# Stage norms of a six-stage fp32 model kernel: inverse deviation by Ln and Exp on ScalarE instead of Sqrt on ScalarE and reciprocal on VectorE

## The reference

```python
def rms_norm(x, g):
    y = xf * lax.rsqrt(jnp.mean(xf * xf, axis=-1, keepdims=True) + NORM_EPS)
    return (y * g)
...
    x = x + pool_mixer(rms_norm(x, pool_norm[j]), ...)          # conv_mixer, mla_mixer alike
    return rms_norm(x, final_norm)                              # end of the first block
...
    h = rms_norm_2(x, mix_pre_norm[l])
    x = x + rms_norm_2(hybrid_token_mixer(h, ...), mix_post_norm[l])
    h = rms_norm_2(x, ffn_pre_norm[l])
    x = x + rms_norm_2(conv_glu_ffn(h, ...), ffn_post_norm[l])
```

## Time and profile before

| | |
|---|---|
| median of 3 executions | 2356.09 us (2353.81 to 2356.2) |
| the profiled execution, its own time | 2356.29 us |
| its span, first to last instruction | 2354.5 us |
| mean granted TensorE clock | 0.981 |
| TensorE busy | 2269.4 us (96%) |
| VectorE busy | 1206.3 us (51%) |
| ScalarE busy | 886.3 us (38%) |
| GpSimd busy | 1031.4 us (44%) |
| instructions | 32284 |

### The profile page before, as it was taken

The page is one execution under the profiler, slowest core; times in us unless marked ns, Lnnn a source line. Parts: engine busy times, 40 slices in busy tenths (PEclk is TensorE's granted clock), DMA queues, the critical chain, the costliest instruction groups (busy, mean ns, idle before and its releaser), DMA issues.

```text
span 2354.5 us, 32284 instructions
## 1 busy us (share of the span) xinstructions
PE 2269.4 (96%) x10448; PEld 1816.3 (77%) x10448; DVE 1206.3 (51%) x1573; ACT 886.3 (38%) x1546; POOL 1031.4 (44%) x753
## 2 busy tenths in 40 slices
PE   8999999999999999999999999989999887999996
PEld 6788888888888887777887888776896565777785
DVE  7832234444432635555267223496754348888613
ACT  4343343344343434444333443334423323323322
POOL 5654444544544444443456544443200032555553
PEclk9999999999999999999999999999999889999998
DMA  3332323233222222111322322222100021222332
GB/s 133 98 99 98 98 91 99 96 98 98 98 96 96 95 93 72 54 63 36 99 90 89 107 98 93 101 89 72 55 1 1 1 72 45 90 97 89 102 104 98
DMA packets 53643, 194.46 MB, mean 83 GB/s; under 512 B 6080, under 2 KB 6336, under 8 KB 53568
## 3 DMA queue, kind: packets, MB, share of 16 engines
q1 hardware_dynamic: 52560, 191.13, 24.8%
q10 hardware_dynamic: 1008, 2.33, 0.3%
HBM read 191.34 MB, written 2.10 MB: 82 GB/s over the span
## 4 chain that ended last, share of the span: by engine, by line
PE 49%; issue 35%; POOL 15%; DVE 1%; POOLq 1%; ACT 0%; ACTq 0%; DVEq 0%
POOL w_lo L569 15%; PE proj L626 13%; PE proj L627 13%; PE proj L628 13%; PE aux L771 1%; PE proj L796 1%; PE proj L725 1%; PE proj L727 1%; PE proj L726 1%; PE aux L774 1%; PE aux L782 1%; PE proj L753 0%; PE proj L755 0%; PE proj L754 0%; PE proj L743 0%
## 5 line engine op out<-in xcount | busy, mean ns | idle before, releaser
L569 POOL TENSOR_TENSOR w_lo<-w_stage,w_hi 128x512 fp32r<-128x512 f32 x716 | 990.4, 1392 | 1226.1 <-ACT w_hi L1152 1225.5
L1152 ACT ACTIVATE w_hi<-w_stage 128x512 fp32r<-128x512 f32 x716 | 437.1, 627 | 761.9 <-PE proj L628 706.3
L626 PE MATMUL proj<-xh,w_hi 128*128 128x512 f32 x1696 | 672.6, 397 | 19.0 <-POOL w_lo L569 16.9
L627 PE MATMUL proj<-xl,w_hi 128*128 128x512 f32 x1696 | 662.0, 390 | 0.0
L628 PE MATMUL proj<-xh,w_lo 128*128 128x512 f32 x1696 | 661.8, 390 | 0.0
L626 PEld LDWEIGHTS proj<-xh,w_hi 128*128 128x128 f32 x1696 | 319.3, 188 | 106.0 <-POOL w_lo L569 34.1
L628 PEld LDWEIGHTS proj<-xh,w_lo 128*128 128x128 f32 x1696 | 319.1, 188 | 67.6
L627 PEld LDWEIGHTS proj<-xl,w_hi 128*128 128x128 f32 x1696 | 319.5, 188 | 66.8 <-issue 2.4
L626 PE MATMUL proj<-act_h,w_hi 128*128 128x512 f32 (+1 forms) x864 | 337.7, 391 | 0.6 <-POOL w_lo L569 0.6
L627 PE MATMUL proj<-act_l,w_hi 128*128 128x512 f32 (+1 forms) x864 | 336.9, 390 | 0.0
L628 PE MATMUL proj<-act_h,w_lo 128*128 128x512 f32 (+1 forms) x864 | 336.9, 390 | 0.0
(11 more groups left out here) (313 smaller groups left out, 2413.4 us busy)
## 6 DMA issues: line engine op xcount, KB each, us to landing
w_stage<-stream SPq DMA_DIRECT2D x358, 512.0 KB, 3.3
out<-x_res SPq DMA_DIRECT2D x4, 512.0 KB, 2.6
x_res<-x SPq DMA_DIRECT2D x2, 512.0 KB, 8.3
consts_sb<-consts ACTq DMA_DIRECT2D x1, 832.0 KB, 4.4
x_res<-x ACTq DMA_DIRECT2D x1, 512.0 KB, 7.4
x_res<-x SPq DMA_DIRECT2D x1, 256.0 KB, 3.3
x_res<-x ACTq DMA_DIRECT2D x1, 256.0 KB, 5.1
pos_i<-pos ACTq DMA_DIRECT2D x1, 256.0 KB, 2.7
```

Of the source, the lines that this page charges most:

```text
L569: pool.tensor_tensor(w_lo[:, at, :], w_stage[:, at, :], w_hi[:, at, :].bitcast(F32), ALU.subtract).then_inc(stage_free, 1)
L626: pe.matmul(o, w_hi[:, slot, cols], hi, start=(b == 0), stop=False)
L627: pe.matmul(o, w_hi[:, slot, cols], lo, start=False, stop=False)
L1152: act.activation(w_hi[:, u % RING, :], w_stage[:, u % RING, :], ACT.Copy).then_inc(hi_done, 1)
```

## The change

All nine places of `deviation` compute exp(-0.5 * ln(sum/D + eps)) on ScalarE. ScalarE's Ln writes std (or r_final), a new semaphore log_done orders the Exp behind it, the Exp writes rstd (or r_final in place) and raises std_done. VectorE's nine reciprocals are gone; its wait on std_done stays. Ahead of each wait for the sum ScalarE runs an Ln of one element per partition (warm).

```diff
                 if ahead:
                     his(4)
+                act.activation(warm[:, :], ones[:, 0:1], ACT.Ln)
                 if twice:
                     stds.up()
                     act.wait_ge(stat_done, stds.n)
-                    act.activation(std[:, :], aux[:, 1, :], ACT.Sqrt, bias=con("eps2"), scale=1.0 / D).then_inc(std_done, 1)
+                    act.activation(std[:, :], aux[:, 1, :], ACT.Ln, bias=con("eps2"), scale=1.0 / D).then_inc(log_done, 1)
+                    act.wait_ge(log_done, logs.up())
+                    act.activation(rstd[:, :], std[:, :], ACT.Exp, scale=-0.5).then_inc(std_done, 1)
                     stds.up()
                     act.wait_ge(stat_done, stds.n)
-                    act.activation(r_final[:, :], aux[:, 0, :], ACT.Sqrt, bias=con("eps"), scale=1.0 / D).then_inc(std_done, 1)
+                    act.activation(r_final[:, :], aux[:, 0, :], ACT.Ln, bias=con("eps"), scale=1.0 / D).then_inc(log_done, 1)
+                    act.wait_ge(log_done, logs.up())
+                    act.activation(r_final[:, :], r_final[:, :], ACT.Exp, scale=-0.5).then_inc(std_done, 1)
                     return
                 stds.up()
                 act.wait_ge(stat_done, stds.n)
-                act.activation(std[:, :], aux[:, 0, :], ACT.Sqrt, bias=con("eps"), scale=1.0 / D).then_inc(std_done, 1)
+                act.activation(std[:, :], aux[:, 0, :], ACT.Ln, bias=con("eps"), scale=1.0 / D).then_inc(log_done, 1)
+                act.wait_ge(log_done, logs.up())
+                act.activation(rstd[:, :], std[:, :], ACT.Exp, scale=-0.5).then_inc(std_done, 1)
...
                     stds.up()
                     dve.wait_ge(std_done, stds.n)
-                    link(dve.reciprocal(rstd[:, :], std[:, :]))
...
                 dve.wait_ge(std_done, stds.n)
-                link(dve.reciprocal(rstd[:, :], std[:, :]))
...
                     if c == 0:
                         dve.wait_ge(std_done, stds.n)
-                        link(dve.reciprocal(r_final[:, :], r_final[:, :]))
```

More of the change, by code:

```diff
@@ L411, in program @@
         std_done = sem("std_done")
+        log_done = sem("log_done")
         prod_done = sem("prod_done")
@@ L1139, in _ @@
             unit, tile = Count(), Count()
+            logs = Count()
             sqs, hs, stds, als, prods, silus, gates, xs = (Count() for _ in range(8))
```

## The result

The changed kernel was faster by more than forecast. In the first six executions of each kernel it took 2342.01 us (2341.6 to 2347.8) and the kernel before 2355.12 us: ratio 0.995, 95% interval 0.9937 to 0.9963, a gain of 13.1 us where 4.5 were forecast, and outside the range of 2347.0 to 2355.5. Over the whole study the changed kernel ran 20 times (median 2343.24) and the kernel before 90 times (median 2355.83): 12.6 us. The profiled execution took 2341.6 us, span 2339.4, granted clock 0.983.

A forecast was written before the change was run, and what follows sets the result against it. TensorE, busy 96% of the span, was taken as the bound. Gains of 1.45 + 1.45 + 1.8 + 1.0 less losses of 0.3, 0.7 and 0.2 gave 4.5 us: 2351.6 against 2356.09, range 2347 to 2355.5.

The forecast's parts named there:

- The price of a place: At each norm, from Ln's start to the first use of rstd: 2.72 us instead of 4.17, so rstd 1.45 earlier.
- at the end and behind the mixer: Norms at the kernel's end and behind the mixer: rstd comes earlier, a gain of 1.45 us at each.
- rival D: A switch of table sets costs another 1.28 us in whole-tile paths; slower, 2362.5 us; chance 0.05.
- rival E: The change doesn't do what it says, or one table load serves both functions; given no chance.
- pool0, pool1, conv, mla, mixer start: Norms of these stages: gain 1.0 us in pool0; losses 0.3 in pool1, 0.7 in conv, 0.2 in mixer; mla 0.
- Rival B: GpSimd's pairs do not give gains back: pool0 gives 2.7, pool1, mixer and ffn 1.4 each; 2345 us; chance 0.11.
- C: ScalarE's later weight units starve TensorE more: mixer 1.5, conv 1.2, pool1 and mla 0.5 each; 2354 us; chance 0.09.
- ffn: Norm of the ffn stage: earlier rstd offset by GpSimd's pair holding up VectorE; 0, bounds -0.3 and +1.4 us.
- r_final in chunk 0: First attention pair: TensorE's 1.83 us wait for softmax probabilities queued behind VectorE's reciprocal goes; gain 1.8 us.
- Rival A: In the chunks, TensorE's full clock returns sooner without the wait; worth 1 to 3.5, say 2.5 us: 2349.1; chance 0.20.
- P: Theory from the experiments: whether the clock falls at chunk 0 depends on when TensorE's short waits come, not on the reciprocal.

The follow-up runs named there:

- before_late: The kernel before plus extra matmuls filling TensorE's idle times at chunk 0 and in and behind the last chunk, no other change: 2347.23 us.
- after_late: The changed kernel plus extra matmuls filling TensorE's idle times at chunk 0 and in and behind the last chunk: 2335.68 us.
- all_but_r_final: The changed kernel with Sqrt and VectorE's reciprocal kept for r_final alone: 2351.62 us.
- after_again: The changed kernel as it is, run again for a second profile and more executions: 2345.66 us.
- before_again: The kernel before as it is, run again for a second profile: 2350.17 us in one execution.
- first_four: The kernel before with Ln and Exp at pool0, conv, mla and pool1 alone: 2355.18 us.
- before_pad1: The kernel before with the first head's products for wt made twice, 0.9 us more TensorE work just ahead of chunk 0: 2351.73 us.
- six_late: The changed kernel with Sqrt and reciprocal kept at conv, mla and pool1, and extra matmuls in TensorE's idle times at chunk 0 and the last chunk: 2334.05 us.

## Why the prediction was wrong

**The price of a place: right.** 2.73 measured for 2.72; 1.43 at the end and behind the mixer for 1.45; none of the new loads has a gap above 0.02 us. That settles rival D: the 1.38 us of drain in the Trainium skill, ScalarE: Activation LUTs, section What ACT_TABLE_LOAD costs, shows nowhere here, and the two loads of every place exclude rival E. The 13 more loads are there (72 against 59).

**pool0, pool1, conv, mla, mixer start: right in kind and nearly in size.** pool0 gave 1.3 by the load and 0.2 to 0.3 by the earlier first tile, 1.5 for my 1.0; the first mark itself scatters by 1 to 2 us between profiles of one form (28.4 to 29.6 with the reciprocal, 27.1 to 29.0 without), so the 1.98 of the two profiles is no better measure. pool1 lost 0.2 for 0.3. Conv lost 0.92 for 0.7, the same in every profile of either form. Rival B is refuted in pool0 by the 3.53 us behind the pair, and C came only at conv. The mixer's first tiles started 1.7 us later behind their mark, and by chunk 0 nothing of that was left.

**ffn: mis-sized.** From ffn's mark to the end's, eight profiles with the reciprocal take 362.94 on average, twelve without it 361.75: 1.2 us, where I took 0 with 1.4 as the bound. The traces show a third of it: GpSimd's pair does hold up VectorE's next steps, but by 1.05 of the 1.45 us (0.81 and 1.54 us where the kernel before has 0.55 and 0.75), so the first prod starts 10.68 us behind the mark, not 11.09, and TensorE's long wait ends 0.4 earlier. The rest comes later in the stage and stays open.

**r_final in chunk 0: this is the step that failed.** I wrote "Gain 1.8: the wait, not the whole 3.35". The wait of 1.83 had been read in a stretch at clock 0.50, where TensorE's own work was so slow that it covered 2 us of VectorE's lateness. At full clock the same wait is 3.8 us, and 0.4 of it are left without the reciprocal. And it was not free of consequences: in its last microsecond or just behind it the clock falls. So where the early fall is absent the reciprocal costs 6.8 to 7.0 us (before_late against after_late, all_but_r_final against after). With the early fall in both it costs 1.1 to 1.2 by chunk 2 (table above), less than my 1.8, because in the low stretch, which lasts 20.5 us either way, TensorE then works at half speed where it had waited. By the stage's end the difference is 5.8 (421.0 and 420.8 against 415.0 and 415.2), since 4.6 more come at the end of the chunks; windows of before

```profile
1859.00:1865.00 6.00, 6.00 (x8) 0.50 0.00 0
1869.00:1875.00 6.00, 4.80 (x24) 0.50 0.01 3
```

and of after_again, both with the early fall:

```profile
1859.00:1865.00 6.00, 3.72 (x29) 0.98 0.00 0
1869.00:1875.00 6.00, 1.94 (x18) 1.00 0.00 0
```

Why one microsecond of place changes the falls there so much I can't derive from rows. before_again, with the reciprocal, has the short form of this stretch too, so I can't call these 4.6 a price of the reciprocal.

**Rival A had the right resource and the wrong mechanism.** I let the clock come back sooner and priced that 1 to 3.5. It does not come back sooner: in after_again the low stretch is as long as before, 1755.6 to 1776.0. What changes is whether it falls. The change moved the first chunk by 0.9 us, and the early fall became rarer. That the 0.9 us did it is P's view, and only partly shown: first_four moved the chunk by half of that and had the fall, before_pad1 moved it the other way and had not. If the fall, worth 3.9 by the stage's end, went from nearly every execution to about half of them, that is 0.5 x 3.9 = 2.0. No case of mine had that, since I asked only what is behind the wait and not what had started the low clock, 8 us ahead of it.

**The sum again**, from measured terms and one estimate: pool0 1.5, conv -0.9, pool1 -0.2, behind the mixer 1.4, ffn 1.2, end 1.4, r_final with the fall 5.8, fewer early falls 2.0: 12.2 us, against 12.6 between the medians of all executions. The last term is the estimate: the share of executions with the fall is read from groups of times with one to three profiles each. With the fall in 59 to 87 of the 90 executions before (the group at 2353.5 to 2354.7 may lack it) and in 7 to 10 of the 20 after, it is 0.6 to 2.4. For the one pair of profiles of the result no share is needed: of the 9.7 us in the mixer 9.6 stand by chunk 2 (273.6 and 264.0), 1.1 for the reciprocal's wait beside the early fall and 8.4 for the fall itself.

## What to carry to other kernels

Before you price a wait of TensorE, look at the granted clock of that stretch. A wait read at half clock is too short by what the slow work covers, and a wait of some microseconds at full clock can cost as much again in the low clock behind it. And look where the low stretch begins: what made it lies ahead of that point, and idle times of 0.3 to 0.75 us were enough here; with these and the one behind them filled by four matmuls of 0.4 to 0.9 us into an unused bank, no profile has the fall. Where such a fall is in play, a shift of a microsecond may be worth more than the edit; compare versions with those gaps filled, or over many executions, and not by six. And when two profiles differ in a low stretch, measure right behind it: at the end of the stage a later stretch had taken half of the difference back. The version for use is six_late: the new form where VectorE or the end waits for rstd, the old one at conv, mla and pool1, and the idle times filled.

## What was unexpected

The granted clock fell in one execution of a kernel and not in another at the same place, with TensorE's work at the same time of the span within 0.1 us (1752.33 and 1752.28 for the same matmul in after and after_again). The Trainium skill, TensorE: Matmul & The Clock Gate, Part 1, says that the chip's watch over TensorE's activity runs free and does not start anew with the kernel; this agrees. But the outcome is not a mere draw: of the kernel before three in 90 executions were below 2352, and with 0.9 us more work ahead of the chunks seven in ten; these are counts of times, since few executions have a profile.

The times of one kernel lie in groups, not around a mean. Part of that does not come from the chunks: in eight of the twenty profiles the clock also falls for 3.4 us in the mla stage at about 1113, and in these, and no others, that stage is 1.1 to 1.5 us longer. The groups are, for the kernel before at 2353.5 to 2354.7, 2355.4 to 2356.7, 2358, 2361.5 and 2364, the changed one at 2342, 2344, 2346 and 2348. A median over six executions moved by 2 us for that reason (2342.01, 2345.66 and 2343.97, measured at three times).
